# A list of 187 unread matrix products in the rest behind the down projection, in place of three

## The reference

```python
def conv_gated_ffn(h, w_gate, w_up, w_conv, w_down):
    g = causal_dwconv(h @ w_gate, w_conv)
    return (jax.nn.silu(g) * (h @ w_up)) @ w_down
...
        f = conv_gated_ffn(rmsnorm(h, g_pre_ffn[layer]), w_gate[layer], w_up[layer],
                           w_ffn_conv[layer], w_down[layer])
        h = h + rmsnorm(f, g_post_ffn[layer])
```

```python
        h = rmsnorm_2(x, norm_mix_g[l])
        proj = jnp.einsum('bsd,de->bse', h, w_in[l])
```

## Time and profile before

| | us |
|---|---|
| two runs | 3168.8 and 3176.8 |
| median | 3172.8 |
| span of the profiled execution | 3175.1 |
| last TensorE record ends | 3166.8 |
| TensorE busy | 3161.9 |
| VectorE busy | 2145.4 |
| ScalarE busy | 1822.0 |
| GpSimd busy | 458.6 |
| HBM read | 601.27 MB, 196 GB/s |

### The profile page before, as it was taken

The page is one execution under the profiler, slowest core; times in us unless marked ns, Lnnn a source line. Parts: engine busy times, 40 slices in busy tenths (PEclk is TensorE's granted clock), DMA queues, the critical chain, the costliest instruction groups (busy, mean ns, idle before and its releaser), DMA issues.

```text
span 3175.1 us, 58846 instructions
## 1 busy us (share of the span) xinstructions
PE 3161.9 (100%) x24159; PEld 3014.4 (95%) x24159; DVE 2145.4 (68%) x3496; ACT 1822.0 (57%) x2608; POOL 458.6 (14%) x321
## 2 busy tenths in 40 slices
PE   9999999999999999999999999999999999999998
PEld 9999999999999999999999999999999888888887
DVE  7987486666664477665666799755555666668776
ACT  6566464444444455545455488877777544445555
POOL 0001200000000100000000057777760000000000
PEclk9999999999999999999999999999999999999999
DMA  6444557666666656545556577787876777766554
GB/s 226 150 144 136 181 183 234 227 225 230 228 200 195 191 174 207 164 153 167 187 193 196 200 190 197 194 193 194 194 195 198 242 242 242 242 224 223 189 191 166
DMA packets 229420, 627.78 MB, mean 198 GB/s; under 512 B 59328, under 2 KB 78624, under 8 KB 229024
## 3 DMA queue, kind: packets, MB, share of 16 engines
q1 hardware_dynamic: 192144, 623.60, 60.3%
q0 software_dynamic: 36864, 0.15, 3.3%
q10 hardware_dynamic: 144, 0.26, 0.0%
HBM read 601.27 MB, written 21.10 MB: 196 GB/s over the span
## 4 chain that ended last, share of the span: by engine, by line
PE 98%; DVE 1%; ACT 0%; DMA 0%; issue 0%; POOL 0%; SPq 0%; DVEq 0%; ACTq 0%; POOLq 0%
PE ps L983 32%; PE ps L984 31%; PE ps L985 31%; PE ps L1056 0%; DVE wl L1553 0%; PE ps L1257 0%; PE ps L1277 0%; PE ps L1280 0%; PE ps L1024 0%; PE ps L1453 0%; PE ps L1281 0%; PE ps L1291 0%; DMA raw<-in_in1k 0%; PE ps L1109 0%; PE ps L1058 0%
## 5 line engine op out<-in xcount | busy, mean ns | idle before, releaser
L2398 ACT CAST wh<-raw 128x1024 fp32r<-128x1024 f32 (+3 forms) x1096 | 1139.0, 1040 | 1029.4 <-PE ps L985 1011.6
L1553 DVE TENSOR_TENSOR wl<-raw,wh 128x1024 fp32r<-128x1024 f32 (+2 forms) x865 | 1039.8, 1203 | 381.8 <-ACT wh L2398 376.6
L983 PE MATMUL ps<-xh,wh 128*128 128x256 f32 x3088 | 854.7, 277 | 0.5 <-issue 0.5
L985 PE MATMUL ps<-xh,wl 128*128 128x256 f32 x3088 | 850.0, 275 | 0.0
L984 PE MATMUL ps<-xl,wh 128*128 128x256 f32 x3088 | 849.8, 275 | 0.0
L983 PE MATMUL ps<-xw,wh 128*128 128x258 f32 (+2 forms) x2096 | 591.5, 282 | 2.0 <-issue 1.1
L985 PE MATMUL ps<-xw,wl 128*128 128x258 f32 (+2 forms) x2096 | 587.7, 280 | 0.0
L983 PEld LDWEIGHTS ps<-xh,wh 128*128 128x128 f32 x3088 | 579.8, 188 | 4.3 <-issue 1.6
L984 PEld LDWEIGHTS ps<-xl,wh 128*128 128x128 f32 x3088 | 579.8, 188 | 1.1 <-issue 1.0
L985 PEld LDWEIGHTS ps<-xh,wl 128*128 128x128 f32 x3088 | 579.7, 188 | 0.0
L2933 POOL DMA_INDIRECT table<-w_loose x256 | 398.3, 1556 | 808.7 <-DVE w_loose L2233 655.6
(11 more groups left out here) (425 smaller groups left out, 4675.9 us busy)
## 6 DMA issues: line engine op xcount, KB each, us to landing
raw<-in_peer_u SPq DMA_DIRECT2D x256, 512.0 KB
raw<-in_peer_v SPq DMA_DIRECT2D x238, 512.0 KB
raw<-in_w_in SPq DMA_DIRECT2D x172, 512.0 KB
raw<-in_w_up SPq DMA_DIRECT2D x82, 512.0 KB
raw<-in_w_gate SPq DMA_DIRECT2D x80, 512.0 KB
raw<-in_w_down SPq DMA_DIRECT2D x80, 512.0 KB
raw<-in_w_out SPq DMA_DIRECT2D x64, 512.0 KB
table<-tmp SPq DMA_DIRECT2D x32, 512.0 KB, 6.4
```

Of the source, the lines that this page charges most:

```text
L983: t.matmul(o, lh, rh, start=start, stop=False)
L985: return t.matmul(o, ll, rh, start=False, stop=stop)
L1553: v.tensor_tensor(part_at(wl, i), raw[:, i % RN, 0:cols(i)], high.bitcast(F32), ALU.subtract).then_inc(lo, 1)
L2398: last = s.copy(part_at(wh, i), raw[:, i % RN, 0:cols(i)])
```

## The change

In the rest, the three products of ones in front of `spread_factor` (`keep_busy(ps[6][:, 0:128], 3)`) are taken out, and a function `unread_forms` stands in their place. It issues 187 products into the banks `ps[4]` and `ps[5]`, whose contents nobody reads before the next stage overwrites them. All are in fp32r on `ah` and `al` with a full 128 x 128 stationary operand, but for eight in bfloat16:

- `products` in nine widths, 512, 128, 64, 384, 320, 448, 272, 258 and 256, four times `three` in each, so 108 products;
- four pairs: one of 512 columns whose moving operand is read in two stretches of 256 columns (a tile of `ah` and the same tile of `al`), and one of 256 columns;
- eight in bfloat16 of 512 columns, where the 128 columns of `identb` are read four times over;
- nine of 128, 130, ... 144 columns, each followed by six of 512 columns.

```diff
--- before.py
+++ after.py
@@ -1002,6 +1002,29 @@
                 last = three(o, row_at(wh, i, k - k0), row_at(wl, i, k - k0), *rhs(k), start and k == k0, stop and k == k0 + n - 1)
             last.then_inc(gemm, 1)
 
+        def unread_forms():
+
+            def flat(half, k, n):
+                o = PAD_A + half * FT * S + 512 * k
+                return ahl[:, o:o + n]
+
+            def products(o, n, times):
+                for k in range(times):
+                    three(o[:, 0:n], ah[:, k, 0:128], al[:, k, 0:128], flat(0, k, n), flat(1, k, n), True, True)
+
+            for n in (512, 128, 64, 384, 320, 448, 272, 258, 256):
+                products(ps[4], n, 4)
+            for k in range(4):
+                both = ahl[:, PAD_A:PAD_A + 2 * FT * S].rearrange("p (h k t) -> p h k t", h=2, t=S)[:, :, k, :]
+                t.matmul(ps[5][:].rearrange("p (h t) -> p h t", h=2), ah[:, k, 0:128], both, start=True, stop=True)
+                t.matmul(ps[5][:, 0:256], al[:, k, 0:128], ah[:, k, :], start=True, stop=True)
+            for k in range(8):
+                t.matmul(ps[5][:].rearrange("p (a b) -> p a b", a=4), identb[:], identb[:].unsqueeze(1).to_broadcast([128, 4, 128]),
+                         start=True, stop=True)
+            for i in range(9):
+                t.matmul(ps[4][:, 0:128 + 2 * i], ah[:, 0, 0:128], flat(0, 0, 128 + 2 * i), start=True, stop=True)
+                products(ps[4], 512, 2)
+
         def token_squares(T, row):
 
             for b, (c, n) in enumerate(blocks(T)):
@@ -1213,7 +1236,7 @@
         token_squares(S, 0)
         t.wait_ge(o_sq, 32)
         token_squares(S, 5)
-        keep_busy(ps[6][:, 0:128], 3)
+        unread_forms()
         spread_factor(S, 3)
         keep_busy(ps[6][:, 0:128], 8)
```

## The result

The changed kernel took 3200.42 us (two runs, 3200.21 and 3200.63), against 3172.8 us before: 27.6 us more, a ratio of 1.008 with a 95% interval from 1.0062 to 1.0097. The forecast was 3206 us, with a range from 3198 to 3215 us. Run again five times beside fifteen runs of the kernel before, it gave a ratio of 1.0083 (1.0068 to 1.0098).

A forecast was written before the change was run, and what follows sets the result against it. TensorE was taken to bound the kernel; 187 products summed to 34.56 us, less the 1.13 us they fill, so 33.4 us on a median of 3172.8 us: 3206.2 us, range 3198 to 3215 us.

The forecast's parts named there:

- What bounds the kernel: Whole kernel: TensorE, busy 3161.9 of 3175.1 us, so added product time is kernel time unless it fills a gap.
- TensorE's last record lies 33 us later: End of the profile with the change: TensorE's last record 33 us later, with no new wait behind 1180 us.
- The stretch that the list fills: In front of `spread_factor`, 1139.75 to 1140.88 us: 1.13 us, the three products of ones and 0.21 us idle, filled for nothing.
- the narrow fp32r product: In the list: 0.22 us for 128 columns, as in plain float32, 0.11 us for 64, 0.234 us for 136 on average.
- rival 1: Narrow fp32r products in the list go at the load's pace: 31.0 us added, 3203.8 us; chance 0.36.
- The two-stretch read: The list's four pairs: 0.226 us like a plain read of 512 columns, at most twice that (+0.9 us).
- the bfloat16 product: Eight in the list: 0.226 us each, taken from the fp32r row; its own row gave 0.216 us; at most twice (+1.8 us).
- Rival 2: Last part of the list: 54 wide products behind narrow ones cost 0.86 us each, 34 us more, 3240 us; chance 0.04.
- Rival 3: In the list, read patterns and odd sizes cost their upper bounds, up to 3211 us; chance 0.08.
- Rival 4: The list's 66 wide products are paced by the load, 0.11 us: 7.7 us less, 3198.5 us; chance 0.02.
- The other engines: During the list: nothing of theirs hangs on it; VectorE and ScalarE cast weights until three buffers are full, then stop.
- a fuller stock of weights: First projection behind the rest, 315 products: more weights already cast could give back 0.3 us.

## Why the prediction was right, and where its terms were off

**What bounds the kernel** was right. With one list TensorE is 31.5 us late behind the rest, with two 64.1 us, and where the last stage has the same pace as in the trace before, that stays within 1 us up to the end. The sign that TensorE's last record lies 33 us later did not come as said: it lies 23.5 us later, since this trace has the faster pace in the last stage. In the second trace of the changed kernel, whose last stage is as slow as before, it lies 32.3 us later.

**The stretch that the list fills** was put at 1.13 us. With `spread_factor` at 1172.52 us in place of 1140.88, the list of 32.82 us costs 31.6 us, so the stretch is 1.2 us. The list behind `spread_factor` confirms the way of counting at another place.

**The terms of the sum**, in us:

| | forecast | measured |
|---|---|---|
| 512 columns | 2.72 | 2.86 |
| 448, 384, 320 | 6.12 | 6.39 |
| 272, 258, 256 | 4.26 | 4.34 |
| 128 columns | 2.64 | 1.28 |
| 64 columns | 1.32 | 1.31 |
| pairs | 1.36 | 1.39 |
| bfloat16 | 1.81 | 1.55 |
| narrow ones with 54 wide ones | 14.33 | 13.70 |
| the list | 34.56 | 32.82 |

The line between the last two parts is not sharp: the last bfloat16 product shows 0.03 us from start to start in place of 0.216, and the narrow product behind it 0.25 us in place of 0.06. Together they took 15.25 us, 16.14 us in the forecast.

The one term that was mis-sized is the narrow fp32r product. The prediction took "the nearest row in width and in element size", plain float32 of 128 columns; measured is the load's pace, 0.11 us, as rival 1 had it (31.0 us of delay, 3203.8 us). The nearer row was the product of one column with its four-byte load, since it shares what bounds a narrow product. That is 2.4 us too much. The fp32r products of 256 and more columns, 0.2315 us in place of 0.2264 at 512, take 0.8 us of it back. The two-stretch read costs nothing (0.232 us, as a plain one at this place), and the bfloat16 product went at 0.216 us, the value that its own row gave and that the prediction passed over; that is the last 0.1 us of the 1.7 by which the list was shorter.

**The rivals.** Rival 2 (wide products hurt by narrow ones) is out: they go at 0.231 us, with one of 0.28 us behind each narrow one, which itself takes 0.06 us from start to start but for the first. Rival 3's forms cost 0.3 us more than forecast for 320 to 448 columns, and less for bfloat16. Rival 4 is out, and with it the 131 ns that the Trainium skill gives for a stream of 512 columns with its loads ("TensorE: Matmul & The Clock Gate", "Back-to-back issue gap"): no row of twelve 512-column fp32r products in any of the fourteen traces went below 0.226 us each.

**The other engines** had nothing to add. The 0.3 us that a fuller stock of weights might have given back did not come.

**The time.** 3200.4 us measured against 3206.2 has two parts. About 1.8 us are the sum (31.6 in place of 33.4). The other 4.0 us are the base: the median of before, 3172.8 us, was the mean of a run at each of two levels 8 us apart, and both runs after fell on the lower. Level against level the kernels are 31.5 to 32 us apart, and the prediction's own scatter of 4 us to either side had room for that. That both runs fell on the lower level is chance: of the five later ones two lie at 3209 us, which is in the range as well.

What stays open is what makes a run take one level or the other. In all traces with the old places of the operands the two levels part at one place of the last stage, where pair sums of the other engines begin and VectorE starts on the remainder `wl` of a chunk. But what these engines do there is no different: in six traces with the slow pace and four with the fast one, their instructions start within 0.02 us of the same distance from TensorE's. The share of the lower level was 5 of 17, 5 of 15, 5 of 11 and 9 of 11 in four sets of runs of the same kernel, each on another chip.

## What to carry to other kernels

In these runs a narrow fp32r product cost the load of its stationary operand (0.112 us for 128 columns), and a wide one its columns (0.44 to 0.47 ns each); take the greater, and look for the row that shares the bound, not the one that looks most alike. Filler work on the bounding engine cost its length less the wait at its place, to 0.2 us, and it can lose the clock without a gap: read the granted clock beside every pace that looks like a new price. When runs of one kernel lie at two levels, compare level with level before reading a small difference, and look for the place where the pace changes by laying two traces over each other.

## What was not expected of the hardware

- The same instructions with the same operands run at 0.2267 or 0.2333 us a product of 512 columns, for nearly 300 us on end, at the same granted clock. Over the last stage this is 8 us, 0.25% of the kernel.
- Moving the stationary operand within its tile, the high part by 4, 16 or 20 columns and the low part by 60, 48 or 44 the other way, changed the pace from 0.2267 to 0.2333, 0.2320 and 0.2342 us, up to 0.7% of the whole kernel's time.
- The granted clock fell to its lower level for 13.7 us under a row of products without a gap, at the end of 36 products of 16, 32 and 64 columns; 24 products of 128 and 64 columns among wide ones, and 187 of 128 columns, left it at the upper level.
- With the three products of ones taken out, TensorE had 0.99 us of idle time between four products of one column and `spread_factor`, and in the one trace of it the clock was at its lower level for the 3.4 us that followed. At a place of the same kind at 405 us, the clock fell for 3.4 us in two of fourteen traces, with those products in place.
